# All groups of two expanding layers from un-normed x, and weight parts made one by one

## What is computed

```python
def rms_norm(x, g):
    y = x * lax.rsqrt(jnp.mean(x * x, axis=-1, keepdims=True) + NORM_EPS)
    return y * g
def modulate(h, shift, scale):
    return h * (1 + scale) + shift
def squared_relu_mlp(h, w1, w2):            # layers 0 and 1, D_FF = 4096
    return jnp.square(jax.nn.relu(h @ w1)) @ w2
def swiglu(h, w_ffn_in, w_ffn_out):         # third block, D_FF_2 = 2816
    a, b = split_cols(h @ w_ffn_in, (D_FF_2, D_FF_2))
    return (jax.nn.silu(a) * b) @ w_ffn_out
...
    x = x + g2 * squared_relu_mlp(modulate(rms_norm(x, norm_mlp[i]), sh2, sc2), mlp_w1[i], mlp_w2[i])
...
    x = x + g2 * swiglu(modulate_2(x, norm2_g[layer], sh2, sc2), w_ffn_in[layer], w_ffn_out[layer])
```

## Time and profile before

| | us |
|---|---|
| median of 3 runs | 1726.2 (1722.22 to 1730.83) |
| the profiled execution | 1725.08 |
| its span, first to last instruction | 1723.3 |
| PE busy in it | 1646.9 (96%) |
| DVE busy | 957.5 (56%) |
| ACT busy | 717.8 (42%) |
| POOL busy | 199.9 (12%) |
| mean granted clock of PE | 0.988 |

### The profile page before, as it was taken

The page is one execution under the profiler, slowest core; times in us unless marked ns, Lnnn a source line. Parts: engine busy times, 40 slices in busy tenths (PEclk is TensorE's granted clock), DMA queues, the critical chain, the costliest instruction groups (busy, mean ns, idle before and its releaser), DMA issues.

```text
span 1723.3 us, 27958 instructions
## 1 busy us (share of the span) xinstructions
PE 1646.9 (96%) x11092; PEld 1318.5 (77%) x11092; DVE 957.5 (56%) x1731; ACT 717.8 (42%) x1330; POOL 199.9 (12%) x245
## 2 busy tenths in 40 slices
PE   5999998999999999999998999999999999989997
PEld 2775446878888888543576899988678899989997
DVE  3444744763444344255755676676667766565554
ACT  3433655441323233233554554455331465344443
POOL 1011432100000001016011000010023400200001
PEclk9999999999999999999998999999999999999999
DMA  9224990332222222433314444543221444445441
GB/s 407 99 98 169 414 358 37 110 136 98 98 98 74 94 77 98 165 150 122 147 47 189 153 153 191 196 150 147 98 98 52 148 147 167 176 147 197 159 166 68
DMA packets 21329, 254.11 MB, mean 147 GB/s; under 512 B 2256, under 2 KB 4560, under 8 KB 5584
## 3 DMA queue, kind: packets, MB, share of 16 engines
q1 hardware_dynamic: 18144, 242.51, 37.1%
q10 hardware_dynamic: 3056, 9.82, 1.5%
HBM read 251.26 MB, written 1.05 MB: 146 GB/s over the span
## 4 chain that ended last, share of the span: by engine, by line
PE 83%; DVE 7%; ACT 4%; issue 2%; DMA 2%; POOL 1%; DVEq 0%; POOLq 0%; ACTq 0%; SPq 0%
PE bank L601 17%; PE bank L602 17%; PE bank L603 17%; PE bank L552 10%; PE bank L674 4%; PE bank L779 3%; PE bank L805 2%; PE bank L1168 2%; PE bank L787 2%; DMA weights<-in_ada 2%; DVE w_lo L2048 2%; PE bank L1141 1%; ACT w_hi L1477 1%; PE bank L754 1%; PE bank L762 1%
## 5 line engine op out<-in xcount | busy, mean ns | idle before, releaser
L1477 ACT ACTIVATE w_hi<-weights 128x1024 fp32r<-128x1024 f32 (+2 forms) x286 | 288.9, 1013 | 250.9 <-PE bank L603 237.6
L2048 DVE TENSOR_TENSOR w_lo<-weights,w_hi 128x1024 fp32r<-128x1024 f32 (+2 forms) x286 | 331.8, 1168 | 80.5 <-ACT w_hi L1477 77.3
L601 PE MATMUL bank<-h_hi,w_hi 128*128 128x256 f32 (+1 forms) x944 | 318.5, 337 | 23.7 <-DVE h_lo L2069 12.0
L603 PE MATMUL bank<-h_hi,w_lo 128*128 128x256 f32 (+1 forms) x944 | 314.5, 333 | 0.0
L602 PE MATMUL bank<-h_lo,w_hi 128*128 128x256 f32 (+1 forms) x880 | 289.6, 329 | 0.0
L601 PEld LDWEIGHTS bank<-h_hi,w_hi 128*128 128x128 f32 x944 | 181.0, 192 | 48.4 <-issue 28.0
L603 PEld LDWEIGHTS bank<-h_hi,w_lo 128*128 128x128 f32 x944 | 181.0, 192 | 18.3
L602 PEld LDWEIGHTS bank<-h_lo,w_hi 128*128 128x128 f32 x880 | 169.3, 192 | 15.0
L601 PE MATMUL bank<-mlp_hidden_hi,w_hi 128*128 128x512 f32 (+1 forms) x512 | 173.6, 339 | 0.9 <-DVE w_lo L2048 0.8
L602 PE MATMUL bank<-mlp_hidden_lo,w_hi 128*128 128x512 f32 (+1 forms) x512 | 173.2, 338 | 0.0
L603 PE MATMUL bank<-mlp_hidden_hi,w_lo 128*128 128x512 f32 (+1 forms) x512 | 173.2, 338 | 0.0
(11 more groups left out here) (330 smaller groups left out, 2940.2 us busy)
## 6 DMA issues: line engine op xcount, KB each, us to landing
weights<-in_ada SPq DMA_DIRECT2D x36, 2048.0 KB, 9.4
weights<-in_mlp_up SPq DMA_DIRECT2D x16, 2048.0 KB, 8.1
weights<-in_mlp_down SPq DMA_DIRECT2D x16, 2048.0 KB, 7.6
weights<-in_ffn_in SPq DMA_DIRECT2D x11, 2048.0 KB, 7.6
weights<-in_in SPq DMA_DIRECT2D x8, 2048.0 KB, 7.6
weights<-in_gate SPq DMA_DIRECT2D x6, 2048.0 KB, 7.6
weights<-in_ffn_out SPq DMA_DIRECT2D x8, 1408.0 KB, 6.0
weights<-in_even_in SPq DMA_DIRECT2D x3, 2048.0 KB, 12.6
```

The source lines that it names most:

```text
L601: mm(out, wh, hi(k), start=k == 0, stop=False)
L603: return mm(out, wl, hi(k), start=False, stop=k == kc - 1)
L1477: A(split_part(w_hi, q), raw_part(q), ACT.Copy).then_inc(sem("w_hi_ready"), 1)
L2048: V.tensor_tensor(split_part(w_lo, q), raw_part(q), split_part(w_hi, q).bitcast(F32), ALU.subtract)\
```

## The change

All 32 groups of mlp1 and all 44 of ffn are early groups; `split_norm` and its steps go there, and h_hi and h_lo of these stages with them. In DVE's ffn loop the making of parts moves behind `early_scale`. In mlp1 the square and `rest` of a group come one iteration later than before. The three presplit parts are made one each at chunks 2, 3 and 4. The modulation block of mlp0 and of mlp1 moves from the norm's sum to behind the second group. In mlp0 one part is made earlier on ACT and DVE. Two tensors lie elsewhere in memory. In the diff below the order is: constants, PE's `early` and `mlp`, PE's entry of ffn, ACT's `norm`, ACT's entry of ffn (mlp1's alike), DVE's `mlp`.

```diff
-        relu["mlp1"] = arena[:, relu_at:relu_at + 3 * LAT].rearrange("p (a b) -> p a b", b=LAT)
+        relu["mlp1"] = h[:, 0:3, 0:LAT]
...
-        EARLY = {"mlp0": 2, "mlp1": 4, "ffn": 2}
-        EARLY_GROUPS = {"mlp0": 2, "mlp1": 4, "ffn": 4}
+        EARLY = {"mlp0": 2, "mlp1": FF // P, "ffn": FF2 // P}
...
+                def fill_ada(m):
+                    if m == 1:
+                        ada_block()
+
                 def up(q):
+                    if n == 1:
+                        early("mlp1", "mlp_up1", range(8 * q, 8 * q + 8), fill_ada)
+                        return
+                    begun = early("mlp0", "mlp_up0", range(EARLY["mlp0"]), fill_ada) if q == 0 else None
...
-            begun = early("ffn", "ffn_in", False)
-            split_linear("ffn_in", range(11), lambda k: h_hi[:, k, 0:LAT], lambda k: h_lo[:, k, 0:LAT], LAT,
...
+            early("ffn", "ffn_in", range(44))
...
-                    if c == 5 and presplit:
-                        split_until(split[0] + presplit)
+                    if 2 <= c < 2 + presplit:
+                        split_until(split[0] + 1)
...
-            norm("ffn", LAT, lambda e, c: drained(e, ("o2", c)), None, PARTS, late=1, early=2)
-            split_until(split[0] + 1)
-            split_norm("ffn", LAT, 2, 24, lat_steps("ffn", "ffn_in", ACT.Silu))
-            mlp("ffn", LAT, ACT.Silu, parts_before("ffn_out"), ahead=2)
+            norm("ffn", LAT, lambda e, c: drained(e, ("o2", c)), None, PARTS, early=2)
+            mlp("ffn", LAT, ACT.Silu, parts_before("ffn_out"))
...
+                def square(f):
+                    a = relu[name][:, f % 3, 0:width]
+                    for s in range(width // LAT):
+                        drained(dve, early_tag(*up_tags(name, f)[0], s, width // LAT))
+                    V.tensor_tensor(a, a, a, ALU.mult).then_inc(sem(f"{name}_full"), 1)
...
-                        split_until(min(end, PART_END[tb] + PARTS - 1))
+                        if name != "ffn":
+                            split_until(min(end, PART_END[tb] + PARTS - 1))
                         a = relu[name][:, i % 3, 0:width]
                         if ahead <= i < EARLY[name]:
-                            early_scale(name, ta[0], i, width)
+                            if i >= 3:
+                                dve.wait_ge(sem(f"{name}_hid"), i - 2)
+                            early_scale(name, ta, i, width)
+                            if name == "mlp0":
+                                split_until(split[0] + 1)
+                            if name == "ffn":
+                                split_until(min(end, PART_END[tb] + PARTS - 1))
+                        if name == "mlp1":
+                            if i % 8:
+                                square(i - 1)
+                            if i % 8 == 7:
+                                square(i)
+                            if i % 8 > 1:
+                                rest(i - 2)
+                            if i % 8 == 7:
+                                rest(i - 1)
+                                rest(i)
+                            continue
                         filled(dve, tb)
```

## The result

| | before | after |
|---|---|---|
| median, us | 1725.22 (4 runs, 1722.22 to 1730.83) | 1760.57 (4 runs, 1758.01 to 1769.25) |
| the profiled execution | 1725.08 | 1758.01 |
| its span | 1723.3 | 1756.2 |
| mean granted clock | 0.988 | 0.986 |

The ratio is 1.021, with an interval of 1.0164 to 1.0255: slower by 35, forecast 27.5, inside the range.

The account below looks back on a forecast made before the run. The prediction took PE to bound the kernel (83% of its chain of work); ffn +36.7, mlp1 -5.0 and mlp0 -4.2 sum to +27.5, added to 1725.1 for about 1753 us. Likeliest case 1744 to 1762; eight-in-ten range 1736 to 1776.

Parts of the forecast that it names:

- The waits in ffn: PE waits in ffn for DVE's `w_lo`, two per block of four groups: 21 waits, 43.2 us of ffn's +36.7.
- either kind: ffn: waits ahead of group 4b+1, 2.06 us each, and waits ahead of group 4b+4, 2.07 each.
- the clock falls: Rival, .20: ffn's 21 waits bring PE to half clock; 1765 for a third of the waits, 1788 for all.
- the likeliest case: Whole kernel at full clock, +27.5 to 1753 us; 1744 to 1762, chance .64.
- a third of the waits: 1765: ffn, within the clock rival of .20: low clock costs 1.7 us behind a third of the waits, giving 1765.
- mlp1: Stage mlp1: 7.6 gained up to the second down group, 2.6 given back later; net -5.0, between -2 and -7.
- mlp0: Stage mlp0: root 1.85 earlier, wait of 3.48 and low clock behind it go; net -4.2, between -1 and -5.
- wait A: ffn, from group 4b's end to group 4b+1's first matmul: DVE's copy stands ahead of the needed `w_lo`; 2.06 us.
- The gain up to the second down group: mlp1: second down group starts at 983.4 against 991.00, 7.6 gained; waits of 3.96 and 2.80 go.
- what is given back later: mlp1, after the second down group: 16 groups x .055 and two more turns at .9, 2.6 us.
- The size of an early group: mlp1 and ffn: .121 us a matmul at 258 columns, .119 at 256; an early group costs .055 more.
- Faster than before: Rival, .08: ffn's parts lie ready in time, PE never stands, ffn ends 6.4 early; 1709 us.

Follow-up runs that it names:

- the longer wait A: Kernel whose only ffn waits are the ten ahead of group 4b+1, with the `w_lo` that ends each made twice by DVE: 1748.38 us (1.0143).
- all that helped: Changed kernel with no waits in ffn, presplit parts made at once, and mlp1's parts at its turns made earlier: 1701.25 us (.9856).
- the two kernels with one kind: Changed kernel with ffn's parts moved earlier so that only waits ahead of group 4b+4 stay: 1727.55 us; only those ahead of 4b+1: 1727.66 us.
- the two runs: Version without waits in ffn, with mlp0's modulation block back in the norm's sum: 1709.88 us; with mlp0's earlier part left out: 1710.43 us.
- the version without waits: Changed kernel with both edits to ffn's order of parts, so all 44 early groups have parts made in time: 1707.12 us (.9911).
- the two versions with the edited turns: Version without waits in ffn, with mlp1's next part made earlier at each eight up groups: 1703.00 us; the same plus presplit at once: 1701.25 us.

## Why the prediction was right, and where it was off

- **The waits in ffn: right in number, place, length and cause.** 21 of them, 1.99 each for 2.06; taking either kind away took away only that kind. That the forecast came out 7 low is not theirs.
- **The clock: the step that failed.** The forecast gave "the clock falls" a chance of .20 and let the likeliest case run at full clock. It fell behind 8 of 21 waits, 11.1 us, which is the miss in ffn (47.2 for 36.7; the waits came out 1.5 shorter and the groups .9 longer). The rival's own line "a third of the waits: 1765" was close, at 1.4 each for 1.7. That 1760.6 still lies within 1744 to 1762, the likeliest case at full clock, is luck: mlp1, mlp0 and the stages without a change came out 5.1 shorter than forecast. The reason against the low clock rested on one wait of 2.24 with full clock behind it; one wait can't speak for 21. It can't even speak for itself: the same wait, 2.23 to 2.25 long, stands in all twelve traces, and in two of them (the longer wait A, and all that helped) the clock falls behind it. Here is the latter:

```profile
300.21 0.47 PE L600 MATMUL bank<-h_hi,w_hi 128*128 128x512 f32 x1 [2.23 <-DVE w_lo L2045]
...
301.69 0.63 PE L600 MATMUL bank<-h_hi,w_hi 128*128 128x512 f32 x1
```

Only 3 of the 21 single waits in the two kernels with one kind are followed by low clock, and 8 of 21 where both kinds stand 5 to 6 us apart. What else decides, at equal length, stays open. The Trainium skill, "TensorE: Matmul & The Clock Gate", section "A second HAM failure mode: psum-queue depth-cycling", tells of a clock that swings because PE stands often between groups; the trace agrees, with a mean clock of .92 in ffn and 8 swings, and 1.00 in ffn once the waits are gone.
- **mlp1:** -6.3 for -5.0; the same instructions took .7 more to 1.0 less in the other traces, so half of this miss could be chance. The gain up to the second down group was 6.8 for 7.6; what is given back later was .5 for 2.6. That term was mis-sized: it took the ordinary groups of before as free of small waits, and the early groups as .055 dearer. Eight up groups took 24.4 and 23.1 us before, and 23.8 and 22.8 after (8 x 2.85 is 22.8).
- **mlp0:** -5.0 up to the first down matmul for -4.2, split as the two runs show; another 1.3 behind it has another source (below). **Elsewhere** the two executions differ by 1.7 where nothing was changed; the stretch between mlp0 and mlp1, which no experiment edits, takes from 220.2 to 226.8 us in the twelve traces.
- **The size of an early group:** .1210 a matmul in the sum, from one stretch, for .1187 at 256 columns. That was no price of two columns. In the version without waits the same early matmul takes one of two distances, for whole groups: in ffn 72 of them from 1530.50 to 1539.06 are .1189 apart, and 72 from 1554.16 to 1562.86 .1208. In mlp1 all 192 of the last eight up groups are .1189 apart:

```profile
1046.03 0.28 PE L721 MATMUL bank<-mlp_early_hi,w_hi 128*128 128x258 f32 x1
...
1068.85 0.32 PE L600 MATMUL bank<-mlp_hidden_hi,w_hi 128*128 128x256 f32 x1
```

What chooses between the two was not tried. The term is small here (2.2 in ffn, .9 in mlp1). The Trainium skill's formula (same page, "Back-to-back issue gap"), which the page gives for a matmul by itself and not for a stream with weight loads, would make two columns .8 ns; next to two distances 1.9 ns apart these rows do not tell.
- **Faster than before** as a rival was worked out at 1709 for parts in time; the run with that order gave 1707.

## What to carry to other kernels

An instruction that waits for the newest result of the busiest engine must not stand ahead of the work that this engine needs next. Ask of every instruction moved in a queue: what does it wait for, and who waits for what stands behind it; the waits that follow can be summed from the trace of before. And where a change makes PE stand again and again, add the low clock behind some of the waits, since its cost here was a quarter of that of the waits.

## What the runs showed of the hardware

- The half clock need not begin with the first matmul behind a wait. In ffn it began 1.3 us after PE had started again, ten matmuls into the group (1531.70 for a wait that ended at 1530.42), so the first matmul's .36 does not tell. Behind the waits of 3.96 and 4.50 of before the first one already lasts .55; behind that of 2.80, which the forecast put with them, the first lasts .36, and the half clock begins .6 us later:

```profile
959.76 0.41 PE L602 MATMUL bank<-h_lo,w_hi 128*128 128x256 f32 x1
```

- In mlp0 the same matmuls at clock 1.00 took one of two times, from the first down matmul to the next norm's sum: 316.4 us before and in the two versions with the edited turns, 315.1 in the changed kernel and the eight other versions. The distance of the matmuls differs by 1 ns all through. So 1.3 of mlp0's 6.3 are not shown to be the change's; why there are two was not tried.
